# Mixer kernel on one core: stage 2 written out and its chunk widened, the low-rank projection of stage 1 divided over column groups

## The reference, cut to what matters

```python
# layer 1: low rank 16, the product with w_alpha gives the gates of 512 channels
q, k, v, g_lr, r = split(h @ w_in)
log_a = log_sigmoid(g_lr @ w_alpha + b_alpha) / GLA_TAU
# layer 2, mLSTM branch, M_CHUNK = 64, four heads of 96
b = cumsum(log_f); g = b[..., -1]
dmat = where(causal, b[:, None] - b[None, :] + log_i, -inf)
m_t = maximum(b + m, max(dmat))
num = exp(b + m - m_t) * (C @ q) + (q @ k.T * exp(dmat - m_t)) @ v
den = ...                      # the same with n and a row of ones
h = num / maximum(abs(den), exp(-m_t))
C_next = exp(g + m - m_next) * C + sum(ws * v k.T)      # likewise n and m
# beside it: window attention over 128 keys with sinks, and stick-breaking attention
y = concat([y_m, y_a, y_s]) @ w_out; x = x + gate * rmsnorm(y, g_post)
```

## Time and profile before

| | us |
|---|---|
| median of 3 runs | 2543.21 (2543.1 to 2544.49) |
| profiled execution | 2537.89 |
| its span, first to last instruction | 2536.1 |
| TensorE busy | 2265.1 (89%) |
| VectorE busy | 1548.6 (61%) |
| ScalarE busy | 1051.0 (41%) |
| GpSimd busy | 566.2 (22%) |

### The profile page before, as it was taken

The page is one execution under the profiler, slowest core; times in us unless marked ns, Lnnn a source line. Parts: engine busy times, 40 slices in busy tenths (PEclk is TensorE's granted clock), DMA queues, the critical chain, the costliest instruction groups (busy, mean ns, idle before and its releaser), DMA issues. The chain is left out here.

```text
span 2536.1 us, 51678 instructions
## 1 busy us (share of the span) xinstructions
PE 2265.1 (89%) x21042; PEld 1624.9 (64%) x21042; DVE 1548.6 (61%) x2486; ACT 1051.0 (41%) x2294; POOL 566.2 (22%) x540
## 2 busy tenths in 40 slices
PE   1799999999999981699999999999998399898988
PEld 1576666666666741699898889898997144343333
DVE  6644444443334435567666666666676698888885
ACT  2333333333334322323232222232233388787875
POOL 0600000100000003132333323232323232332331
PEclk9999999999999995899999999999999599999999
DMA  9300000000000007100000000000000802111111
GB/s 397 104 18 18 18 26 18 26 18 18 26 18 18 26 9 296 75 30 25 27 29 29 27 25 26 26 25 25 28 27 16 275 24 67 50 59 59 59 51 50
DMA packets 82220, 138.71 MB, mean 55 GB/s; under 512 B 42433, under 2 KB 63041, under 8 KB 77905
## 3 DMA queue, kind: packets, MB, share of 16 engines
q1 hardware_dynamic: 82000, 135.38, 15.2%
HBM read 103.89 MB, written 31.46 MB: 53 GB/s over the span
## 5 line engine op out<-in xcount | busy, mean ns | idle before, releaser
L1315 PE MATMUL m_bank<-m_arena,m_w_hi 128*128 128x128 bf16 (+1 forms) x2688 | 476.3, 224 | 35.0 <-DVE m_w_lo L1287 20.5
L1316 PE MATMUL m_bank<-m_arena,m_w_hi 128*128 128x128 bf16 (+1 forms) x2688 | 475.9, 221 | 0.0
L1317 PE MATMUL m_bank<-m_arena,m_w_lo 128*128 128x128 bf16 (+1 forms) x2688 | 475.7, 222 | 0.0
L1315 PEld LDWEIGHTS m_bank<-m_arena,m_w_hi 128*128 128x128 bf16 (+1 forms) x2688 | 261.4, 97 | 43.2 <-DVE m_w_lo L1287 20.9
L1316 PEld LDWEIGHTS m_bank<-m_arena,m_w_hi 128*128 128x128 bf16 (+1 forms) x2688 | 266.6, 99 | 0.2
L1317 PEld LDWEIGHTS m_bank<-m_arena,m_w_lo 128*128 128x128 bf16 (+1 forms) x2688 | 260.1, 97 | 0.0
L1705 POOL TENSOR_TENSOR s_hi<-s_sp,s_cols 128x512 bf16<-128x512 f32 x144 | 152.3, 1057 | 364.8 <-DVE s_sp L1836 155.3
L217 POOL TENSOR_TENSOR g_stage<-g_stage,g_nh_row 128x1024 f32<-128x1024 f32 x16 | 52.3, 3269 | 751.0 <-DVE g_stage L486 751.0
L552 PE MATMUL g_bank<-g_h_hi,g_wi_hi 128*128 128x128 bf16 (+1 forms) x1152 | 197.2, 220 | 18.9 <-DVE g_wi_lo L504 18.7
L553 PE MATMUL g_bank<-g_h_lo,g_wi_hi 128*128 128x128 bf16 (+1 forms) x1152 | 196.8, 220 | 0.0
L554 PE MATMUL g_bank<-g_h_hi,g_wi_lo 128*128 128x128 bf16 (+1 forms) x1152 | 196.8, 220 | 0.0
(11 more groups left out here) (357 smaller groups left out, 5663.5 us busy)
## 6 DMA issues: line engine op xcount, KB each, us to landing
m_arena<-in_w_in_dram SPq DMA_DIRECT2D x8, 1604.0 KB, 7.9
g_stage<-in_gla_w_in_dram SPq DMA_DIRECT2D x8, 1544.0 KB, 12.6
g_stage<-in_ada_w_dram SPq DMA_DIRECT2D x8, 1536.0 KB, 11.2
g_xs<-in_x_dram SPq DMA_DIRECT2D x16, 512.0 KB, 3.2
x<-g_stage SPq DMA_DIRECT2D x16, 512.0 KB, 2.7
m_arena<-in_w_mod_dram SPq DMA_DIRECT2D x8, 1024.0 KB, 7.0
m_arena<-x SPq DMA_DIRECT2D x16, 512.0 KB, 3.7
s_xr<-x SPq DMA_DIRECT2D x16, 512.0 KB, 4.1
```

Source lines behind the costliest of these rows:

```text
L1315: pe.matmul(out, l_hi, r_hi, start=(k == 0), stop=False)
L1316: pe.matmul(out, l_hi, r_lo, start=False, stop=False)
L1317: ins = pe.matmul(out, l_lo, r_hi, start=False, stop=(k == n - 1))
```

## The change

In stage 1 the low-rank part of w_in is padded from 16 to 32 columns with zeros. The eight blocks of the contraction are divided over four column groups of 32: block kb goes to group kb mod 4, so four partial sums stand in the partitions 0 to 127 of A. w_alpha is stacked four times (each padded to 32 rows), and the alpha product over 128 rows adds the parts.

In stage 2 the loops are written out on all engines. The gates i and f are one product of 36 columns (f begins at row 32). The mLSTM has a chunk of 128 tokens, so there is one kv, one inter and one state update a tile, and masks and scans lose their break at 64. turn_x stands right behind kv and writes its second half to bank B5 instead of G0; TensorE waits for hf_done ahead of the window scores, which write B5. x_stats and x_norm stand earlier, and the state update stands behind h_make.

```diff
+            def low_rank():
+                cs = slice(A0, A0 + GA)
+                for half in range(2):
+                    for l, r in ((wi_hi, h_hi), (wi_hi, h_lo), (wi_lo, h_hi)):
+                        for j in range(4):
+                            kb = 4 * half + j
+                            ins = pe.matmul(A[j * GA:(j + 1) * GA, 0:T], l[:, kb, cs], r[:, kb, :],
+                                            start=(half == 0 and l is wi_hi and r is h_hi), stop=(half == 1 and l is wi_lo),
+                                            skip_group_check=True, tile_position=(0, j * GA))
+                ins.then_inc(s["glr_done"], 1)
-                by_feature(A[0:GR, 0:T], A0, GR, "glr_done")
+                low_rank()
-                act.activation(glr[:], A[0:GR, 0:T], ACT.Copy).then_inc(s["glr_copied"], 1)
+                act.activation(glr[:], A[:, 0:T], ACT.Copy).then_inc(s["glr_copied"], 1)
...
+        def all_tiles(tile):
+            for i in range(NT):
+                tile(i, i % 2, i // 2, i == 0, i == NT - 1)
...
-                for n, name in enumerate(("i", "f")):
-                    cs = slice(C0[name], C0[name] + MH)
-                    mm3(TR[0:MH, n * T:(n + 1) * T], ..., "gates_done" if n else None)
+                cs = slice(C0["i"], C0["i"] + FROW + MH)
+                mm3(TR[0:FROW + MH, 0:T], ..., "gates_done")
...
-                kv(0, B3)
+                pe.wait_ge(s["ktok_copied"], i + 1)
+                pe.wait_ge(s["vw_done"], i + 1)
+                for h in range(MH):
+                    ins = pe.matmul(B3[0:MD, h * (MD + 1):(h + 1) * (MD + 1)], k_tok[:, h, :], vw[:, h, :],
+                                    start=True, stop=True)
+                ins.then_inc(s["kv_done"], 1)
+                if not last:
+                    turn_x(i + 1)
                 pe.wait_ge(s["az_read"], i + 1)
                 by_feature(G0, [(C0["sz"] + n * P, P) for n in range(2)], "sz_done")
-                inter(0)
-                kv(1, B5)
-                if not last:
-                    turn_x(i + 1)
+                wait("state_done", i)
+                for h in range(MH):
+                    ins = pe.matmul(B4[:, h * (MD + 1):(h + 1) * (MD + 1)], qT[0:MD, h, :], C_st[par][0:MD, h, :],
+                                    start=True, stop=True)
+                ins.then_inc(s["inter_done"], 1)
                 pe.wait_ge(s["sqk_copied"], 2 * (i + 1))
                 by_token(G1, C0["sv"], SW, "sv_done")
-                pe.wait_ge(s["state_done"], NC * i + 1)
-                inter(1).then_inc(s["inter_done"], 1)
                 pe.wait_ge(s["dx_done"], i + 1)
...
-                pe.wait_ge(s["state_done"], NC * (i + 1))
+                pe.wait_ge(s["state_done"], i + 1)
+                if not last:
+                    pe.wait_ge(s["hf_done"], 2 * (i + 2))
```

More of the change, by code:

```diff
@@ L1053, in tile @@
                 act.activation(av[:, par, :], G1[:, MW:MW + AKV * AD], ACT.Copy).then_inc(s["tv_copied"], 1)
+                if not last:
+                    x_stats(i + 1, 1 - par, half + par, link)
                 act.wait_ge(s["cols_done"], i + 1)
@@ L1102, in _ @@
             act.wait_ge(s["tiles_free"], 1)
[L1103 to L1109, removed]
+            all_tiles(tile)
             late(NT - 1, 1)
@@ L1187, in tile @@
                 link.done(dve.tensor_tensor(g_r, li, b_r, ALU.subtract))
[L1188 to L1195, removed]
+                m_old, m_new = (m_0, m_1) if par == 0 else (m_1, m_0)
+                link.done(dve.tensor_tensor_scan(m_r, g_r, g_r, m_old[0:MH], ALU.max, ALU.max))
+                link.done(dve.tensor_scalar(wi_r, m_r, -1.0, m_old[0:MH], ALU.mult, ALU.add))
+                link.done(dve.tensor_scalar(ws_r, g_r, m_r[:, T - 1:T], None, ALU.subtract))
+                link.done(dve.tensor_tensor(m_new[0:MH], b_r[:, T - 1:T], m_r[:, T - 1:T], ALU.add))
                 link.done(dve.scalar_tensor_tensor(nm_r, b_r, -1.0, m_r, ALU.mult, ALU.subtract))
@@ L1228, in tile @@
                    .then_inc(s["dx_done"], 1)
[L1229 to L1239, removed]
                 if not last:
                     h_make(i + 1)
+                dve.wait_ge(s["kv_done"], i + 1)
+                old, new = C_st[par], C_st[1 - par]
+                for h in range(MH):
+                    ins = dve.scalar_tensor_tensor(new[0:MD, h, :], old[0:MD, h, :], carry[0:MD, h:h + 1],
+                                                   B3[0:MD, h * (MD + 1):(h + 1) * (MD + 1)], ALU.mult, ALU.add)
+                ins.then_inc(s["state_done"], 1)
+                if not last:
                     h_low(i + 1)
@@ L1302, in _ @@
             dve.wait_ge(s["tiles_free"], 1)
-            all_tiles(dve, tile)
+            all_tiles(tile)
             heads_out(NT - 1, 1)
@@ L1387, in turn_o, with tile @@
                 ins.then_inc(s["oT_done"], 1)
-            def tile(i, par, half, first, last, second=False):
+            def tile(i, par, half, first, last):
+                second = i == 1
                 pe.wait_ge(s["h_lo_done"], i + 1)
-                for n, name in enumerate(("i", "f")):
-                    cs = slice(C0[name], C0[name] + MH)
-                    mm3(TR[0:MH, n * T:(n + 1) * T], [(w_hi[:, kb, cs], w_lo[:, kb, cs], h_hi[:, kb, :], h_lo[:, kb, :])
-                                                      for kb in range(KB)], "gates_done" if n else None)
+                cs = slice(C0["i"], C0["i"] + FROW + MH)
+                mm3(TR[0:FROW + MH, 0:T], [(w_hi[:, kb, cs], w_lo[:, kb, cs], h_hi[:, kb, :], h_lo[:, kb, :])
+                                           for kb in range(KB)], "gates_done")
                 pe.wait_ge(s["hf_done"], 2 * (i + 1))
@@ L1411, in tile @@
                 for h in range(MH):
-                    pe.matmul(TR[0:MD, 4 * MH + NC * h:4 * MH + NC * (h + 1)], sel[:, h, 0:MD],
-                              wi_r[:, CH - 1:T:CH], start=True, stop=True)
+                    pe.matmul(TR[0:MD, 4 * MH + h:4 * MH + h + 1], sel[:, h, 0:MD], wi_r[:, T - 1:T],
+                              start=True, stop=True)
                 for n, row in enumerate((g_r, wi_r, ws_r, nm_r)):
```

79 lines of the change are left out of this document (31 added, 48 removed).

## The result

| | before | changed |
|---|---|---|
| median, us | 2543.4 | 2473.0 |
| runs, us | 2543.1 to 2544.5 | 2468.1 to 2479.8 |
| profiled execution / its span, us | 2537.9 / 2536.1 | 2479.8 / 2478.0 |

The ratio is 0.9724 (95% interval 0.9697 to 0.9752): 70 us less, where 73 were forecast. The runs of the changed kernel lie 12 us apart, those of before 1.4, and the one of the changed kernel that was profiled is the longest of them. That spread is part of what has to be explained.

The account below looks back on a forecast made before the run. TensorE was taken to bound stages 1 and 2, nearly always busy. Gains of 18.1, 52.6 and 23.2 less 20.2 (new wait) and 1.0 (loads) gave 72.7 us, from 2543.2 to 2470 us; range 2458 to 2482 at 0.60.

Parts of the forecast that it names:

- Stage 1, 18.1 us: Stage 1: alpha product 0.29 us and low-rank projection 0.84 us less a tile, over 16 tiles.
- The low-rank term: Stage 1 projection: 24 matmuls in four column groups take 0.60 us instead of 1.44; lower bound 0.43.
- Stage 2 work, 52.6 us: Stage 2 TensorE work: gates 1.36 and chunk of 128 1.93 us less a tile, over 16 tiles.
- The new wait, 20.2 us: Stage 2, ahead of p_times_v: TensorE waits 1.37 us for ScalarE's copies of the probabilities in tiles 2 to 15.
- The written-out loop, 23.2 us: Stage 2: the five loop returns go, 14.9 us, with the low clock behind them, 8.3 us.
- the idle term: Stage 2 loop returns: TensorE's five idle stops, 14.9 us start against start, go.
- 6.4 us lost to low clock: Stage 2, behind the four-row matmuls: four tiles lose 1.6 us each, taken to stay.
- clock in every tile: Stage 2: four-row stretch or new idle costs clock in 11 more tiles, 18 us, 2488; chance 0.11.
- no wait at L1371: Stage 2, p_times_v: the chain finds unseen slack, 20 us more gained, 2450; chance 0.13.
- single file: Stage 1 projection: column groups don't run side by side, 13.4 us don't come, 2484; chance 0.10.
- code that isn't fetched in time: Written-out code: each refill costs 2.9 us; at two a tile 93 us, 2563; chance 0.03.
- The margin named as late next, h_low: Stage 2: VectorE's h_low ends 0.63 us before the next tile's start, with 1.54 before the change.

Follow-up runs that it names:

- e9: The changed kernel with the gates as before, in two groups of 24 matmuls; 2474.7 us, 0.9721 of the kernel before.
- e2: The kernel before with only stage 2 written out on every engine; 2520.6 us, 0.9885 of the kernel before.
- e4: The changed kernel with ScalarE's copies of the turned probabilities ahead of its wait for the gates product; 2447.0 us, 0.9602 of the kernel before.
- e6: The changed kernel with both stage 1 written out and ScalarE's copies of the probabilities first; 2442.7 us, 0.9589 of the kernel before.
- e7: e4 plus 22 unused matmuls ahead of each p_times_v, work in place of the changed kernel's wait; 2463.1 us, 0.9669 of the kernel before.
- e10: e6 with the eight matmuls that spread the negated maxima contracting over 128 rows instead of 4; 2436.4 us, 0.9566 of the kernel before.
- e8: e2 plus the gates in one group of 24 matmuls, chunk still 64; 2499.2 us, 0.9822 of the kernel before.
- e3: The changed kernel with all 24 low-rank matmuls in one column group; 2486.6 us, 0.9754 of the kernel before.
- e5: The changed kernel with stage 1 written out on every engine as well; 2466.0 us, 0.9681 of the kernel before.

## Why the prediction was right, and where it was not

The forecast was 2470, the median 2473.0. It is right in its mechanism, and nearer than its terms deserve: that errors of opposite sign nearly cancel is luck. For the profiled execution the forecast was 2465.2, and the two that were profiled took 2479.8 and 2467.4.

**Stage 1, 18.1 us.** A clean tile lost 1.23 us (1.13 forecast). The low-rank term, 0.84, measured 0.99: the round of four goes at the pace of one narrow matmul, the lower bound of the text. The rest, 0.24 against 0.29, is the product with w_alpha. The Trainium skill (TensorE: Matmul & The Clock Gate, "Wait — 56ns, not 53.3ns?") says that starts are never closer than about 25 ns. Here 24 matmuls with their change of shape took 0.45 us, so this sentence does not hold across column groups. "Nothing else of stage 1 comes up" was wrong: behind the loop's returns come stalls with no release, 4.6 us in all in the first profile (the mean of tiles 1 to 14 is 52.6 where 52.28 is clean) and 2.5 in the second. Before there had been next to none (0.4), with 1.44 us of slow matmuls there. Alone, the part measured 18.

**Stage 2 work, 52.6 us.** Right but 0.2 a tile short: 56.01 - 52.50 is 3.51, where 3.29 was forecast. The inter product of full width goes at 0.92 from start to start, with 0.98 taken.

**The new wait, 20.2 us.** Right: its place, its cause and its size. p_times_v would start at 16.32 (16.30 forecast) and starts at 17.55 (17.67); 1.27 us between clean tiles with and without it, 18 us in all. What the text did not draw from it: with the chunk changed, the gates' part is worth next to nothing, since what they free becomes the wait. e9 shows it, by 0.08 us a tile and 0.9721 to 0.9716.

**The written-out loop, 23.2 us.** 28.8 alone, where the kernel before takes 2549.3; the idle term held (14.3 us of "issue"), the clock behind it was under-sized from one profile.

**The clock, the step that failed.** The text says: "An idle of 1.89 us in stage 3 costs no clock, so I charge none for the new wait." In stage 2 it costs: seven low stretches directly behind it in the first profile, one, two and four in three others with the wait, and none in seven kernels without an idle of that size (e2, e4, e6, e7, e9, e10, and e8 with 0.05 us). What it costs lies between e7 (12 us less without it) and e9 (nothing less without it): with the idle time gone, the stretches behind the four-row matmuls can be as many as both kinds were. The forecast left 6.4 us lost to low clock in place; the first profile lost 17, the second 10. That is what the rival "clock in every tile" said, at some half of its 18 us in the first profile and a fifth in the second. The text also has no term for the low clock behind the last tile, which took 3.2 us more than before in both.

**How the errors add.** Worse than forecast: the clock in the tiles by 4 to 10 us, the clock behind the last tile by 3.2 and the stalls of stage 1 by 2.5 to 4.6. Better: stage 2's work by 3.5, the wait by 2, the clean tile of stage 1 by 1.6, the returns by up to 5.6. Of the other rivals, no wait at L1371 fell with the first profile of the changed kernel, single file with e3, and code that isn't fetched in time with e2 and e5. The margin named as late next, h_low, ends 0.70 us before the next tile and was not reached.

**What stays open.** Which tile has a low stretch. e9 and e7 differ by 0.08 us a tile and have six and two; one kernel had ten and six in two executions. With the gates in two groups of four columns there were five and six without any wait (e2, e9), with one group one to four (e4, e6, e7, e8). Whether the narrow gates add to it, or only shift the tiles in time, was not separated; it bears on what the wait costs. Why the clock stays low for 34.1 us behind the last tile in some kernels (changed, e4, e8, e9) and for 6.8 in others (e3, e5, e6, e7, e10) is open too. That the 12-us spread of the changed kernel's runs comes from these stretches is supported by the two profiled executions, and not shown for the runs that were not profiled.

## What to carry to other kernels

When one change shortens the path to a product and another shortens the cover of the chain that feeds it, add both to the margin before either is booked: here each alone cost 0 to 0.2 us of waiting, and together 1.27, and one of them was worth next to nothing. A consumer's copy should not stand behind a wait for something that it doesn't need; moving three copies ahead of two gave 29 us for no work. A microsecond of idle TensorE is to be priced with the clock behind it, as a range (0 to 12 us for 14 of them here), and short matmuls over few rows with theirs: half of them filled up with rows of zeros cost the same time, and the clock kept up in the one execution that was profiled.

## What the runs showed of the hardware

Matmuls of one round start 2 to 9 ns apart over four column groups, and a round of four takes 0.056 us, what a single one takes. The clock fell after a stretch in which only 4 of the array's rows worked for 2 us, although TensorE was not idle (in one to six of 15 tiles, and in none, in one execution, when its last half had 128 rows). It also fell behind 1.06 us of idle in stage 2 (behind one to six of the 14 waits of an execution), where 1.89 us in stage 3 had left it full. A loop's return costs 2.9 us of idle in stage 2's long body; in stage 1 it costs next to nothing (0.4 us over 14 tiles) with 1.44 us of slow matmuls behind it, and up to 0.75 us a tile when 24 matmuls go in 0.45. The Trainium skill (Runtime: NRT & Kernel Launch, "Instruction fetch mechanics") has a taken branch wait for its instructions and straight code fetched ahead. Both written-out stages agree: no stall in tiles 1 to 14 of stage 1 (e5), and no wait in tiles 2 to 15 of stage 2 (e2).
